# Order of DVE and ACT work around the pairs and levels of the second attention

## The chip, the cores and the metric

The kernel runs on one core of one Trainium2 chip. The metric is the device time in microseconds of one execution, the median of repeated runs. The engines are TensorE (PE), VectorE (DVE), ScalarE (ACT), GpSimd (POOL) and SyncE (SP), which issues the loads.

## The reference

Two transformer-like blocks run one after the other on 256 tokens of width 1024, each with a mixer and an expert layer over 16384 experts. The mixer of the second block is what matters here. It splits one input projection seven ways, into queries, keys and values of a block-sparse attention (8 heads of 64) and query, forget gate, input and output gate of a gated recurrence (4 heads of 128):

```
q_a, k_a, v_a, q_r, f_r, i_r, g_r = jnp.split(proj, IN_SPLITS, axis=-1)
attn = moba_attention(q_a.reshape(B, S, ATTN_HEADS, ATTN_HD),
...
rec = hgrn2(q_r, f_r, i_r, g_r, lb_all[layer], rec_norm_g[layer])
h = h + jnp.concatenate([attn, rec], axis=-1) @ w_out[layer]
```

With 256 tokens there is one attention block, so the attention is a causal softmax with a linear distance penalty. The recurrence is

```
decay = jnp.where(causal[None, None, :, :, None], jnp.exp(jnp.minimum(diff, 0.0)), 0.0)
scores = jnp.einsum('bhtd,bhtsd,bhsd->bhts', qc, decay, kc)
```

with `diff` the difference of cumulated logarithms of the forget gate. Its result is normed per head and multiplied with the opened output gate.

## The kernel before

All products run in float32 as three products of rounded halves. A weight tile of 128x1024 comes into one of four places of `ring`; ACT rounds it into `whi` (`highs_to`, L1232), POOL subtracts to get the rest `wlo` (L568), and PE multiplies high by high, low by high and high by low (L634 to L636). `highs_to(end)` rounds all tiles up to `end` that are not yet rounded; each rounding waits until PE has used the tile four before it. The roundings of slot s feed slot s + 2.

The second attention is the stage of this change. Its input projection has 14 slots (`IN2_SLOTS`): fr, fr, qr, qr, qa, ka, va, qa, ka, va, ir, ir, gr, gr, each of two weight tiles and 48 matmuls of 256 columns on PE. Slots of fr, qr, qa and ka come out as columns and are copied by DVE (L1853); va, ir and gr come out as rows and are copied by ACT (L1355, L1356).

Between the slots stand two chains of small work. **Pairs** (four pairs of heads): `m_scores` makes the scores on PE (L913, L915), DVE adds the penalty (L1862) and takes the maxima (L1864, L1865), ACT does four exponentials (L1364); `m_norm` is a reciprocal on DVE (L1868) and four scalings on ACT (L1371); `m_turn` turns the weights on PE (L924), ACT copies them (L1376); `m_values` multiplies by the values on PE (L888), ACT copies (`chi`, L1379), DVE takes the rest (`clo`, L1857). The turn of a pair waits for the `clo` of the pair before, since both use bank 1 of PSUM. **Levels** (0 to 8, doubling spans of the recurrence): `rec_decay` subtracts on DVE (L1884; level 8 L1887) and, in the same step, does two exponentials on ACT (L1388, L1389; level 8 L1391, L1392); `rec_factors` multiplies queries and keys by them on DVE (L1906, L1907; level 8 L1910, L1911); `rec_level` makes score matmuls in two halves on PE (L941, 16 records; level 8 L947); `rec_take` merges them into `Ssum` on DVE (L1894, twice). Level 8 is copied into `Sx` by ACT (L1395), and `rec_values` (L957, L960) needs `Sx`, all takes and the input slots. Then the norm, the gate (L1927) and the output projection follow.

The order is written out by hand: `schedule2` returns one list of steps, and each engine walks through the same list and emits its own part of each step. There is no scheduler behind it. So a step's place in the list is its place in the queue of each engine that has a part in it, and an instruction that waits holds up everything behind it on its engine. `SCORES_AT` puts the pairs' scores at slots 6, 7, 9 and 11, `LEVEL_AT` the levels 0 to 7 at slots 4 to 11; turn and scalings of a pair come one slot after its scores, its values two slots after.

Of the kernel before, what the change touches and what calls it, by code (L numbers as in the profile page):

```python
# [46 lines left out]
HALVES = KC // KH  # L47
RING = 4
# [40 lines left out]
FIRST, N_SLOTS = {}, 0  # L89
# [65 lines left out]
def schedule2():  # L155

    steps = []
    for s in range(len(IN2_SLOTS)):

        def pairs(late):  # L160
            return [h for h in range(PAIRS) if SCORES_AT[h] + late == s]

        level = s - LEVEL_AT[0] if s in LEVEL_AT else None
        if s == LEVEL_AT[-1] + 1:
            steps.append(("rec_level", 8))
        for h in pairs(1):
            steps.append(("m_norm", h))
        if level is not None:
            steps.append(("rec_factors", level + 1))
        if s == len(IN2_SLOTS) - 1:  # L170
            steps.append(("rec_norm", 0))
            steps.append(("proj_half", s))
            for h in pairs(2):
                steps.append(("m_values", h))
        steps.append(("proj", s))
        if s == 1:
            steps.append(("rec_prep", 0))
        if s == 2:
            steps.append(("rec_sums", 0))
        if s == 3:  # L180
            steps.append(("rec_decay", 1))
        if s < len(IN2_SLOTS) - 1:
            for h in pairs(2):
                steps.append(("m_values", h))
        if level is not None:
            steps.append(("rec_level", level))
            steps.append(("rec_take", level))
        if s == 12:
            steps.append(("rec_values", 0))
        for h in pairs(1):  # L190
            steps.append(("m_turn", h))
        for h in pairs(0):
            steps.append(("m_scores", h))
        if level is not None and level + 2 <= 8:
            steps.append(("rec_decay", level + 2))
    steps.append(("rec_gate", 0))
    return steps


def block_program(nc, weights, const1, const2, gains, keys_in, x, out):  # L200
    with ExitStack() as ctx:
# [299 lines left out]
        def bank(i, a=0, b=512):  # L501
            return ps[:, i, a:b]
# [690 lines left out]
        def _(eng):  # L1193
            steps = [0]
# [26 lines left out]
            def token_scale(t):  # L1221
                return stat[:, 3, t:t + 1]
# [3 lines left out]
            def highs_to(end):  # L1226

                for m in range(split[0], end):
                    eng.wait_ge(slot_in[m % RING], 16 * (m // RING + 1))
                    if m >= RING:  # L1230
                        eng.wait_ge(slot_used, m - RING + 1)
                    eng.activation(whi[:, m % RING, :], ring[:, m % RING, :], ACT.Copy).then_inc(hi_ready[m % RING], 1)  # L1232
                split[0] = end
# [97 lines left out]
            def attention2():  # L1331
                base = FIRST_GATE
                for what, i in schedule2():
                    if what == "proj_half":
                        highs_to(FIRST["in2"] + HALVES * i + 1 + RING)
                    elif what == "proj":
                        name, off = IN2_SLOTS[i]
                        if IN2_COLUMNS[i]:
                            highs_to(FIRST["in2"] + HALVES * (i + 1) + RING)
                            if name in FUNC:  # L1340
                                eng.wait_ge(col_copied, i + 1)
                                dst = colT[name][:, off // P:off // P + 2, :]
                                eng.activation(dst, dst, FUNC[name]).then_inc(fr_open if name == "fr" else qr_open, 1)
                            if name == "fr":
                                if i == 0:
                                    eng.wait_ge(g_lb, 1)
                                eng.wait_ge(fr_open, i + 1)
                                for h in (2 * i, 2 * i + 1):
                                    f = colT["fr"][:, h, :]
                                    eng.activation(f, f, ACT.Identity, bias=lbs[:, 6, h:h + 1], scale=lbs[:, 7, h:h + 1])\  # L1350
                                       .then_inc(fr_bound, 1)
                        else:
                            eng.wait_ge(slot_used, FIRST["in2"] + HALVES * (i + 1))
                            out, func = bank(4 + i % 2).rearrange("p (t c) -> p t c", t=2), FUNC.get(name, ACT.Copy)
                            eng.activation(raw2[name][:, 0, off:off + SC], out[:, 0, :], func, scale=token_scale(0))  # L1355
                            eng.activation(raw2[name][:, 1, off:off + SC], out[:, 1, :], func, scale=token_scale(1))\  # L1356
                               .then_inc(proj_copied, 1)
                            highs_to(FIRST["in2"] + HALVES * (i + 1) + RING)
                    elif what == "m_scores":
                        eng.wait_ge(m_max, i + 1)  # L1360
                        for h in range(2):
# [18 lines left out]
                    elif what == "rec_prep":  # L1380
                        eng.wait_ge(fr_bound, REC_H)
                        eng.activation(dlt.rearrange("p h t c -> p (h t c)"), colT["fr"].rearrange("p h c -> p (h c)"),
                                       ACT.Ln).then_inc(g_log, 1)
                    elif what == "rec_decay":
                        eng.wait_ge(g_dlt, i)
                        if i < 8:
                            v, h = level(dlt, i)
# [861 lines left out]
```

## Time and profile before

| | us |
|---|---|
| median of three runs | 2029.32 |
| lowest, highest | 2029.26, 2030.48 |
| the profiled execution | 2028.86 |
| its span in the profile | 2027.1 |
| window over slots 4 to 13 of the second attention | 94.0 |

The page gives each engine's busy share and the chain that ended last. A window gives busy time in a stretch, so that the gaps of an engine are the difference to its length. A timeline row is an instruction or a run of equal ones in order of time; in brackets stands how long the engine was idle before it and what ended that. PE's ends are modelled, each matmul's tail overlaps the next, so gaps are best read between starts.

### The profile page before, as it was taken

To read this page: it belongs to the slowest core of one execution; us is meant where nothing else is said; L and a number is where in the kernel's file an instruction comes from. 1 tells how busy PE (TensorE), PEld (TensorE's weight loads), DVE (VectorE), ACT (ScalarE), POOL (GpSimd) and SP (SyncE) were. 2 spreads that over 40 slices of the span, in tenths; PEclk is the share of its full clock that TensorE was granted. 3 is DMA by queue.
4 is the path that set the end of the run, shared out by engine and by line. 5 is a ranking of instruction groups with operands and counts; after the bars stand their busy time and mean duration, and the time that the engine had idled before them with its cause. 6 is when DMAs were issued, how large, how long until landed. Compare 5 with 4: busy or idle time off the path is not lost.

```text
span 2027.1 us, 39389 instructions
## 1 busy us (share of the span) xinstructions
PE 2000.8 (99%) x14308; PEld 1794.7 (89%) x14308; DVE 1236.9 (61%) x2093; ACT 1011.5 (50%) x1318; POOL 1420.0 (70%) x592
## 2 busy tenths in 40 slices
PE   8999999999999999999999999999999999999998
PEld 8988999999888888888889899999988888888886
DVE  5246379912776799953336638981276689994333
ACT  5546555454555544445446665444455544444443
POOL 7656878888877877754448467888877887774442
PEclk9999999999999999999999999999999999999999
DMA  7433545555555555565655344555555555555553
GB/s 267 157 126 125 186 150 184 180 183 178 174 172 172 174 173 170 175 224 186 186 187 178 114 146 148 188 184 183 180 166 175 176 170 172 172 169 182 185 187 129
DMA packets 97299, 351.46 MB, mean 173 GB/s; under 512 B 12113, under 2 KB 12369, under 8 KB 96849
## 3 DMA queue, kind: packets, MB, share of 16 engines
q1 hardware_dynamic: 96224, 345.40, 52.2%
q10 hardware_dynamic: 1008, 5.13, 0.7%
q8 instruction: 47, 0.77, 0.2%
q14 instruction: 20, 0.16, 0.0%
HBM read 349.44 MB, written 1.05 MB: 173 GB/s over the span
## 4 chain that ended last, share of the span: by engine, by line
PE 94%; DVE 3%; ACT 2%; issue 1%; DMA 0%; POOL 0%; SPq 0%; ACTq 0%; DVEq 0%; POOLq 0%
PE ps L634 23%; PE ps L636 23%; PE ps L635 23%; PE ps L1053 12%; PE ps L1054 6%; PE ps L1045 3%; PE ps L1029 1%; DVE act L1884 0%; PE ps L602 0%; DVE act L1907 0%; ACT whi L1232 0%; POOL wlo L577 0%; PE ps L779 0%; DVE act L1894 0%; DMA xres<-in_x 0%
## 5 line engine op out<-in xcount | busy, mean ns | idle before, releaser
L568 POOL TENSOR_TENSOR wlo<-ring,whi 128x1024 fp32r<-128x1024 f32 x584 | 1411.8, 2422 | 575.3 <-ACT whi L1421 455.9
L1421 ACT ACTIVATE whi<-ring 128x1024 fp32r<-128x1024 f32 x536 | 566.3, 1060 | 775.1 <-PE ps L636 588.7
L634 PE MATMUL ps<-whi,shi 128*128 128x512 f32 x1024 | 408.6, 399 | 0.0
L636 PE MATMUL ps<-whi,slo 128*128 128x512 f32 x1024 | 405.9, 396 | 0.0
L635 PE MATMUL ps<-wlo,shi 128*128 128x512 f32 x1024 | 405.9, 396 | 0.0
L634 PE MATMUL ps<-hboth,whi 128*128 128x256 f32 x1392 | 395.6, 284 | 0.0
L635 PE MATMUL ps<-hboth,whi 128*128 128x256 f32 x1392 | 393.9, 283 | 0.0
L636 PE MATMUL ps<-hboth,wlo 128*128 128x256 f32 x1392 | 393.9, 283 | 0.0
L1053 PE MATMUL ps<-hboth,whi 128*128 128x512 f32 x1024 | 359.3, 396 | 0.0
L1054 PE MATMUL ps<-hboth,wlo 128*128 128x256 f32 x1024 | 283.7, 277 | 0.0
L634 PEld LDWEIGHTS ps<-hboth,whi 128*128 128x128 f32 x1392 | 267.1, 192 | 1.4 <-issue 0.8
L635 PEld LDWEIGHTS ps<-hboth,whi 128*128 128x128 f32 x1392 | 267.2, 192 | 0.0
L636 PEld LDWEIGHTS ps<-hboth,wlo 128*128 128x128 f32 x1392 | 267.1, 192 | 0.0
L636 PEld LDWEIGHTS ps<-whi,slo 128*128 128x128 f32 x1024 | 192.8, 188 | 46.8
L634 PEld LDWEIGHTS ps<-whi,shi 128*128 128x128 f32 x1024 | 192.9, 188 | 45.6
L635 PEld LDWEIGHTS ps<-wlo,shi 128*128 128x128 f32 x1024 | 193.0, 189 | 45.4
L1053 PEld LDWEIGHTS ps<-hboth,whi 128*128 128x128 f32 x1024 | 192.1, 188 | 43.1
L2057 DVE TENSOR_TENSOR wlo<-ring,whi 128x1024 fp32r<-128x1024 f32 x64 | 79.7, 1245 | 238.0 <-ACT whi L1421 238.0
L2051 DVE TENSOR_TENSOR slo<-act,shi 128x512 fp32r<-128x512 f32 x128 | 183.9, 1437 | 22.4 <-ACT shi L1485 22.4
L1054 PEld LDWEIGHTS ps<-hboth,wlo 128*128 128x128 f32 x1024 | 192.4, 188 | 0.0
L2013 DVE TENSOR_TENSOR work<-iota,ps 128x1024 f16<-128x1024 f16 x128 | 154.9, 1210 | 0.0
L2023 DVE TENSOR_TENSOR act<-ps,act 128x512 f32 (+1 forms) x128 | 86.9, 682 | 95.2 <-PE ps L1045 95.2
(300 smaller groups left out, 2709.2 us busy)
## 6 DMA issues: line engine op xcount, KB each, us to landing
ring<-in_weights SPq DMA_DIRECT2D x651, 512.0 KB, 3.3
act<-in_const ACTq DMA_DIRECT2D x1, 2372.0 KB, 9.1
act<-in_const SPq DMA_DIRECT2D x1, 2240.0 KB, 12.3
xres<-in_x SPq DMA_DIRECT2D x4, 256.0 KB, 4.5
act<-in_keys ACTq DMA_DIRECT2D x1, 1024.0 KB, 4.8
out<-act ACTq DMA_DIRECT2D x2, 512.0 KB, 2.6
ring<-in_weights SPq DMA_DIRECT2D x2, 256.0 KB, 4.7
act<-in_fgain ACTq DMA_DIRECT2D x1, 512.0 KB, 3.5
```

Source lines behind the costliest of these rows:

```text
L568: pool.tensor_tensor(wlo[:, j, :], ring[:, j, :], whi[:, j, :].bitcast(F32), ALU.subtract)\
L634: pe.matmul(dst, wide[0], narrow[0], start=start, stop=False, skip_group_check=True)
L635: pe.matmul(dst, wide[0], narrow[1], start=False, stop=False, skip_group_check=True)
L636: return pe.matmul(dst, wide[1], narrow[0], start=False, stop=stop, skip_group_check=True)
L1045: mm = pe.matmul(bank(6 + c, q * HALF, (q + 1) * HALF), hot2[:, c, q, :], hot1[:, c, w, q, :], start=(q + w == 0), stop=(w == 1), skip_gro ...
L1053: pe.matmul(bank(b), whi[:, j, c], hboth[:, :, kc, :], start=kc == 0, stop=False, skip_group_check=True)
L1054: mm = pe.matmul(bank(b, 0, S), wlo[:, j, c], hhi[:, kc, :], start=False, stop=kc == KC - 1, skip_group_check=True)
L1421: eng.activation(whi[:, j, :], ring[:, j, :], ACT.Copy).then_inc(hi_ready[j], 1)
L2013: eng.tensor_tensor(hot2[:, j], iota[:, :].unsqueeze(1).to_broadcast([P, TOK, NKEY]), over(row(1, at), NKEY), ALU.is_equal)
L2023: eng.tensor_tensor(a, bank(6 + j).rearrange("p (q k) -> p k q", q=TOK), a, ALU.mult)\
L2051: eng.tensor_tensor(slo[:, j, :, :], act[:, bass.ds(p * 2, 2), :], shi[:, j, :, :].bitcast(F32), ALU.subtract)\
L2057: eng.tensor_tensor(wlo[:, j, :], ring[:, j, :], whi[:, j, :].bitcast(F32), ALU.subtract)\
```

## The change

Five steps of `schedule2` get other places. The roundings of a slot (`highs_to`) become a step of their own, `highs`, behind the values of a pair; they used to follow the slot's own copy. `m_norm` moves from the next slot to the end of the slot of its scores. ACT's part of `rec_decay` becomes a step of its own, `rec_exp`, behind the scalings. `rec_factors` of level l + 1 moves from the head of the next slot to behind the take of level l, or, in a slot with scores, to behind them; at level 8 it stands ahead of the scores. The first half of slot 12 moves ahead of level 8 (`proj_half`), and the rounding that belongs to it ahead of the copy of level 8. No instruction is added or taken out.

```diff
--- before.py
+++ after.py
@@ -162,11 +162,8 @@
 
         level = s - LEVEL_AT[0] if s in LEVEL_AT else None
         if s == LEVEL_AT[-1] + 1:
+            steps.append(("proj_half", s))
             steps.append(("rec_level", 8))
-        for h in pairs(1):
-            steps.append(("m_norm", h))
-        if level is not None:
-            steps.append(("rec_factors", level + 1))
         if s == len(IN2_SLOTS) - 1:
             steps.append(("rec_norm", 0))
             steps.append(("proj_half", s))
@@ -179,20 +176,29 @@
             steps.append(("rec_sums", 0))
         if s == 3:
             steps.append(("rec_decay", 1))
+            steps.append(("rec_exp", 1))
         if s < len(IN2_SLOTS) - 1:
             for h in pairs(2):
                 steps.append(("m_values", h))
+        steps.append(("highs", s))
         if level is not None:
             steps.append(("rec_level", level))
             steps.append(("rec_take", level))
         if s == 12:
             steps.append(("rec_values", 0))
+        if level == 7:
+            steps.append(("rec_factors", 8))
         for h in pairs(1):
             steps.append(("m_turn", h))
         for h in pairs(0):
             steps.append(("m_scores", h))
+        if level is not None and level < 7:
+            steps.append(("rec_factors", level + 1))
+        for h in pairs(0):
+            steps.append(("m_norm", h))
         if level is not None and level + 2 <= 8:
             steps.append(("rec_decay", level + 2))
+            steps.append(("rec_exp", level + 2))
     steps.append(("rec_gate", 0))
     return steps
 
@@ -1336,8 +1342,8 @@
                     elif what == "proj":
                         name, off = IN2_SLOTS[i]
                         if IN2_COLUMNS[i]:
-                            highs_to(FIRST["in2"] + HALVES * (i + 1) + RING)
                             if name in FUNC:
+                                highs_to(FIRST["in2"] + HALVES * (i + 1) + RING)
                                 eng.wait_ge(col_copied, i + 1)
                                 dst = colT[name][:, off // P:off // P + 2, :]
                                 eng.activation(dst, dst, FUNC[name]).then_inc(fr_open if name == "fr" else qr_open, 1)
@@ -1355,7 +1361,8 @@
                             eng.activation(raw2[name][:, 0, off:off + SC], out[:, 0, :], func, scale=token_scale(0))
                             eng.activation(raw2[name][:, 1, off:off + SC], out[:, 1, :], func, scale=token_scale(1))\
                                .then_inc(proj_copied, 1)
-                            highs_to(FIRST["in2"] + HALVES * (i + 1) + RING)
+                    elif what == "highs":
+                        highs_to(FIRST["in2"] + HALVES * (i + 1) + RING)
                     elif what == "m_scores":
                         eng.wait_ge(m_max, i + 1)
                         for h in range(2):
@@ -1381,7 +1388,7 @@
                         eng.wait_ge(fr_bound, REC_H)
                         eng.activation(dlt.rearrange("p h t c -> p (h t c)"), colT["fr"].rearrange("p h c -> p (h c)"),
                                        ACT.Ln).then_inc(g_log, 1)
-                    elif what == "rec_decay":
+                    elif what == "rec_exp":
                         eng.wait_ge(g_dlt, i)
                         if i < 8:
                             v, h = level(dlt, i)
```

DVE at slots 5 to 7, before: the decay of level 3 (L1884), the factors of level 3 (L1906, L1907), the take of level 2 (L1894), the scores of pair 0 (L1862 to L1865), the decay of level 4, the reciprocals of pair 0, the factors of level 4.

```order
L1884 TENSOR_TENSOR act<-act 128x1024 [waits rec_level_ready]
L1906 TENSOR_TENSOR act<-act 128x128x4 [waits rec_scores_ready,rec_exp_ready]
L1907 TENSOR_TENSOR act<-act 128x128x4
L1894 COPY_PREDICATED act<-act,ps 128x512 [waits rec_scores_ready] x2
L1862 SCALAR_TENSOR_TENSOR act<-ps,act 128x768 [waits moba_scores_ready]
L1864 TENSOR_REDUCE stat<-act 128x2 [waits dve_step]
L1865 TENSOR_REDUCE stat<-act 128x2
L1884 TENSOR_TENSOR act<-act 128x1024 [waits rec_level_ready]
L1868 RECIPROCAL stat<-stat 128x2x2 [waits moba_exp_ready]
L1906 TENSOR_TENSOR act<-act 128x64x8 [waits rec_scores_ready,rec_exp_ready]
L1907 TENSOR_TENSOR act<-act 128x64x8
```

The same place after (L1891 decay, L1901 take, L1869 to L1872 scores, L1913 and L1914 factors, L1875 reciprocals):

```order
L1891 TENSOR_TENSOR act<-act 128x1024 [waits rec_level_ready]
L1901 COPY_PREDICATED act<-act,ps 128x512 [waits rec_scores_ready] x2
L1869 SCALAR_TENSOR_TENSOR act<-ps,act 128x768 [waits moba_scores_ready]
L1871 TENSOR_REDUCE stat<-act 128x2 [waits dve_step]
L1872 TENSOR_REDUCE stat<-act 128x2
L1913 TENSOR_TENSOR act<-act 128x128x4 [waits rec_scores_ready,rec_exp_ready]
L1914 TENSOR_TENSOR act<-act 128x128x4
L1875 RECIPROCAL stat<-stat 128x2x2 [waits moba_exp_ready]
L1891 TENSOR_TENSOR act<-act 128x1024 [waits rec_level_ready]
```

The factors of level 3 moved from ahead of the take to behind the maxima of pair 0, and the reciprocals ahead of the decay of level 4.

ACT at slots 7 and 8, before: the exponentials of level 5 (L1388, L1389), the scalings of pair 1 (L1371), the roundings of slot 8 (L1232), the copy of pair 0's values (L1379), the copy of pair 1's turned weights (L1376).

```order
L1388 ACTIVATE act<-act 128x32x16 [waits rec_diff_ready]
L1389 ACTIVATE act<-act 128x32x16
L1371 ACTIVATE act<-act,stat 128x128 [waits moba_reciprocal_ready]
L1371 ACTIVATE act<-act,stat 128x256
L1371 ACTIVATE act<-act,stat 128x128
L1371 ACTIVATE act<-act,stat 128x256
L1232 ACTIVATE whi<-ring 128x1024 [waits slot_used,slot_in0]
L1232 ACTIVATE whi<-ring 128x1024 [waits slot_used,slot_in1]
L1379 ACTIVATE chi<-ps 128x256 [waits moba_out_ready]
L1376 ACTIVATE act<-ps 128x768 [waits moba_out_ready,moba_transposed]
```

The same place after (L1378 scalings, L1395 and L1396 exponentials, L1386 values, L1238 roundings, L1383 turned weights):

```order
L1378 ACTIVATE act<-act,stat 128x128 [waits moba_reciprocal_ready]
L1378 ACTIVATE act<-act,stat 128x256
L1378 ACTIVATE act<-act,stat 128x128
L1378 ACTIVATE act<-act,stat 128x256
L1395 ACTIVATE act<-act 128x32x16 [waits rec_diff_ready]
L1396 ACTIVATE act<-act 128x32x16
L1386 ACTIVATE chi<-ps 128x256 [waits moba_out_ready]
L1238 ACTIVATE whi<-ring 128x1024 [waits slot_used,slot_in0]
L1238 ACTIVATE whi<-ring 128x1024 [waits slot_used,slot_in1]
L1383 ACTIVATE act<-ps 128x768 [waits moba_out_ready,moba_transposed]
```

The values' copy now stands ahead of the roundings and right behind the exponentials, which stand behind the scalings.

DVE at slots 10 to 12, before: factors of level 7, take of level 6, decay of level 8 (L1887), factors of level 8 (L1910, L1911), rest of pair 2's values (L1857), take of level 7, scores of pair 3.

```order
L1906 TENSOR_TENSOR act<-act 128x8x64 [waits rec_scores_ready,rec_exp_ready]
L1907 TENSOR_TENSOR act<-act 128x8x64
L1894 COPY_PREDICATED act<-act,ps 128x512 [waits rec_scores_ready] x2
L1887 TENSOR_TENSOR act<-act 128x4x128 [waits rec_level_ready]
L1910 TENSOR_TENSOR act<-act 128x4x128 [waits rec_scores_ready,rec_exp_ready]
L1911 TENSOR_TENSOR act<-act 128x4x128
L1857 TENSOR_TENSOR clo<-ps,chi 128x256 [waits heads_highs_ready]
L1894 COPY_PREDICATED act<-act,ps 128x512 [waits rec_scores_ready] x2
L1862 SCALAR_TENSOR_TENSOR act<-ps,act 128x768 [waits moba_transposed,moba_scores_ready]
L1864 TENSOR_REDUCE stat<-act 128x2 [waits dve_step]
L1865 TENSOR_REDUCE stat<-act 128x2
```

The same place after (L1894 decay of level 8, L1917 and L1918 factors of level 8, L1864 rest of the values):

```order
L1901 COPY_PREDICATED act<-act,ps 128x512 [waits rec_scores_ready] x2
L1913 TENSOR_TENSOR act<-act 128x8x64 [waits rec_scores_ready,rec_exp_ready]
L1914 TENSOR_TENSOR act<-act 128x8x64
L1894 TENSOR_TENSOR act<-act 128x4x128 [waits rec_level_ready]
L1864 TENSOR_TENSOR clo<-ps,chi 128x256 [waits heads_highs_ready]
L1901 COPY_PREDICATED act<-act,ps 128x512 [waits rec_scores_ready] x2
L1917 TENSOR_TENSOR act<-act 128x4x128 [waits rec_scores_ready,rec_exp_ready]
L1918 TENSOR_TENSOR act<-act 128x4x128
L1869 SCALAR_TENSOR_TENSOR act<-ps,act 128x768 [waits moba_transposed,moba_scores_ready]
L1871 TENSOR_REDUCE stat<-act 128x2 [waits dve_step]
L1872 TENSOR_REDUCE stat<-act 128x2
```

The factors of level 8 moved from ahead of the take of level 7 to between it and the scores of pair 3.

## Rows read from the trace of the kernel before

**Rows 1.** the page: busy time of the span, and the chain by engine

```profile
PE 2000.8 (99%) x14308; PEld 1794.7 (89%) x14308; DVE 1236.9 (61%) x2093; ACT 1011.5 (50%) x1318; POOL 1420.0 (70%) x592
...
PE 94%; DVE 3%; ACT 2%; issue 1%; DMA 0%; POOL 0%; SPq 0%; ACTq 0%; DVEq 0%; POOLq 0%
```

**Rows 2.** windows view: us, then busy us of PE, PEld, DVE, ACT, POOL, clock, DMA

```profile
1093.00:1187.00 94.00, 90.97 (x768) 86.93 (x767) 61.40 (x78) 58.73 (x115) 57.43 (x23) 1.00 0.38 125
```

**Rows 3.** PE timeline: start, length, line, operands, count, [idle before, releaser]

```profile
1123.12 1.95 PE L941 MATMUL ps<-act 128*128 128x128 f32 x16
...
1125.76 0.87 PE L924 MATMUL ps<-ident,act 128*128 128x128 f32 x6 [0.70 <-ACT act L1371]
...
1134.16 2.05 PE L941 MATMUL ps<-act 128*128 128x128 f32 x16
...
1137.91 0.84 PE L924 MATMUL ps<-ident,act 128*128 128x128 f32 x6 [1.69 <-DVE clo L1857]
...
1153.92 1.95 PE L941 MATMUL ps<-act 128*128 128x128 f32 x16
...
1155.70 0.82 PE L924 MATMUL ps<-ident,act 128*128 128x128 f32 x6
...
1166.56 1.13 PE L947 MATMUL ps<-act 128*128 128x128 f32 x8 [0.65 <-DVE act L1894]
...
1173.28 1.28 PE L957 MATMUL ps<-act 128*128 128x128 f32 x10
```

**Rows 4.** POOL timeline of the same stage: the low roundings of the slots

```profile
1088.56 24.70 POOL L568 TENSOR_TENSOR wlo<-ring,whi 128x1024 fp32r<-128x1024 f32 x8 [1.45 <-ACT whi L1232]
...
1117.28 2.42 POOL L568 TENSOR_TENSOR wlo<-ring,whi 128x1024 fp32r<-128x1024 f32 x1 [4.02 <-ACT whi L1232]
...
1119.63 2.42 POOL L568 TENSOR_TENSOR wlo<-ring,whi 128x1024 fp32r<-128x1024 f32 x1
...
1146.39 4.74 POOL L568 TENSOR_TENSOR wlo<-ring,whi 128x1024 fp32r<-128x1024 f32 x2 [5.50 <-ACT whi L1232]
...
1157.21 4.77 POOL L568 TENSOR_TENSOR wlo<-ring,whi 128x1024 fp32r<-128x1024 f32 x2 [6.08 <-ACT whi L1232]
```

**Rows 5.** DVE timeline of the same stage: operations with two SBUF inputs

```profile
1108.11 2.87 DVE L1907 TENSOR_TENSOR act<-act 128x512 f32<-128x512 f32 x1
...
1119.93 3.21 DVE L1884 TENSOR_TENSOR act<-act 128x1024 f32<-128x1024 f32 x1
...
1124.96 0.68 DVE L1907 TENSOR_TENSOR act<-act 128x512 f32<-128x512 f32 x1
...
1151.05 1.22 DVE L1884 TENSOR_TENSOR act<-act 128x1024 f32<-128x1024 f32 x1
...
1159.84 2.69 DVE L1910 TENSOR_TENSOR act<-act 128x512 f32<-128x512 f32 x1 [2.60 <-ACT act L1392]
```

**Rows 6.** ACT and DVE timelines: exponentials 3, the maxima of scores 0 and 3

```profile
1114.38 0.63 ACT L1388 ACTIVATE act<-act 128x512 f32<-128x512 f32 x1 [5.84 <-DVE act L1884]
...
1119.33 0.68 DVE L1865 TENSOR_REDUCE stat<-act 128x2 f32<-128x512 f32 x1
...
1166.92 0.94 DVE L1862 SCALAR_TENSOR_TENSOR act<-ps,act 128x768 f32<-128x768 f32 x1
...
1168.23 0.68 DVE L1865 TENSOR_REDUCE stat<-act 128x2 f32<-128x512 f32 x1
```

**Rows 7.** ACT timeline: roundings of slot 8 and the copy of pair 0's values

```profile
1135.05 1.99 ACT L1232 ACTIVATE whi<-ring 128x1024 fp32r<-128x1024 f32 x2
...
1136.94 0.36 ACT L1379 ACTIVATE chi<-ps 128x256 fp32r<-128x256 f32 x1
```

**Rows 8.** ACT timeline: exponentials, cross copy and scalings at pair 3

```profile
1168.94 0.40 ACT L1364 ACTIVATE act<-act,stat 128x128 f32<-128x128 f32 x1 [3.63 <-DVE stat L1865]
...
1170.71 0.58 ACT L1395 ACTIVATE act<-ps 128x512 f32<-128x512 f32 x1
...
1171.19 1.49 ACT L1371 ACTIVATE act<-act,stat 128x128 f32<-128x128 f32 x4
```

## The prediction, made before the run

> **What bounds the kernel now.** I read the page first: TensorE (PE) is busy for 99% of the span and carries 94% of the chain that ended last [rows 1]. A change can therefore only help by closing a gap on PE, and it hurts as soon as it opens one. The change touches nothing but the second attention, so the next view is one window over that stage: 90.97 us of PE work in 94.00 us, at a granted clock of 1.00, the upper of its two levels [rows 2]. There are 3.0 us of gaps, and no more. The PE timeline says where they lie [rows 3]: 0.70 us before the turn of pair 0 (L924), which waits for the pair's scalings on ACT; 1.69 us before the turn of pair 1, which waits for the low rest of pair 0's values (clo) on DVE; 0.65 us before the scores of level 8 (L947), which wait for DVE's take of level 7. Counted from start to start, which also takes in the tail of the last matmul, a level block lasts 1155.70 - 1153.92 = 1.78 us where nothing waits, so the three waits cost 0.9 us (1123.12 to 1125.76), 2.0 us (1134.16 to 1137.91) and 0.65 us: **3.5 us in all, 0.17% of the run**. That is the most that the change can give back. A difference under about 0.2% (4.1 us) can't be told from no change here.
>
> **What the waits of the new order will be made of.** The second thing to read is how DVE and POOL hinder each other. DVE's subtraction of level 7 (L1884) took 1.22 us at 1151.05, when POOL's pair of roundings was ending at 1151.13; the same instruction for level 4 began at 1119.93 and took 3.21 us [rows 5]. POOL's second operation of that pair ran from 1119.63 to 1122.05 [rows 4], and DVE ended 1.1 us after it. The factors L1907 took 0.68 us beside an idle POOL, 2.87 us in the stretch in which POOL was busy without a break (1088.56 to 1113.26), and L1910 began at 1159.84, ended at 1162.53, and POOL's pair ended at 1161.98 [rows 4, 5]. So each of these operations with two inputs in SBUF waits until the POOL operation that is under way is over, and then needs about 0.55 us (512 elements) or 1.1 us (1024). POOL's eight operations in the long stretch lasted 24.70/8 = 3.1 us where 2.4 is usual: it waits for DVE as well. From the 2.87 us of the second of two factors I take that the two engines take turns, POOL's next operation slipping in between two of DVE's.
> The Trainium skill (SBUF — State Buffer, section "SBUF: two separate sides") calls this an exclusive lock on a shared port pair: who starts first keeps it for the whole instruction. The trace agrees. It speaks against this change, and without it the sum would be the gain of the last rival below.
>
> **The change, part by part.** A rounding pair on ACT takes 2.0 us [rows 7], and POOL's pair starts 1.1 us after the first and lasts 4.8 us. In the old order the factors of a level (L1906, L1907) stood at the head of the next slot, before the copy of its product: they ran when the exponentials ended, mostly after POOL's pair (levels 4 to 7 at 0.7 us each). In the new order they stand behind the take and, in a slot with a pair, behind the pair's maxima. That is 3 to 6 us after a slot's products end, just where POOL works on the pair of roundings that the same end released. No instruction is added or removed and no DMA issue moves; what changes is who waits. I carried the rows along the new order: an instruction starts when its engine is free and its releaser done, its length from the rows, port as above. The same working for the old order comes within 0.6 us of the trace at the end of the stage.
> - **Values ahead of the roundings.** Removes one rounding pair, 1.9 us, between the values' matmuls and their copy L1379: it ran at 1136.94, behind roundings from 1135.05 [rows 7]. The roundings are 0.4 us later, and have some 7 us until PE wants them: cost nothing.
> - **Scalings ahead of the exponentials.** Pair 0's scalings no longer stand behind a decay of 3.21 us and two exponentials of 1.2 us. The wait before turn 0 goes.
> - **Factors of level 3 behind scores 0.** First the delay before it: factors 2 and decay 3 now fall into POOL's pair of slot 5. Decay 3 ends at 1116.6 (before: 1114.35), its exponentials at 1117.8, and they hold up the copy of slot 6 and its roundings: POOL starts at 1119.5 instead of 1117.28 [rows 4, 6]. Maxima 0 end at 1119.9, as before (1120.01) [rows 6]. Factor one finds POOL at work until 1121.9, ends at 1122.5; POOL's second operation lasts until 1124.7; factor two ends at 1125.3. Level 3 was reached at 1123.12 [rows 3]: **a new wait of 2.2 us**. The order of the two requests at 1119.5 and 1119.8 is close.
> - **Turn 1.** Factors 4 end at 1134.7, decay 5 at 1136.0, exponentials 5 at 1137.4. Values 0 end at 1135.5, but their copy now stands behind exponentials 5: clo at 1138.1, where level 4 is over at 1137.1. The wait shrinks from 2.0 to **1.0 us** and does not go.
> - **Level 6** (factors behind scores 2, POOL's pair up to 1153.6): factors end 1154.8, PE is there at 1154.1: **0.7 us**, new.
> - **Level 8.** Half a slot of products (2.9 us: level 8 and a whole slot take 1173.28 - 1166.56 = 6.7) now stands ahead of it, which covers the take. But factors 8 come after take 7, not at 1159.84. Roundings 11 start at 1164.5, POOL at 1165.6; factor one asks at 1166.7 and ends at 1168.6, POOL's second operation at 1170.8, factor two at 1171.4. PE is through at 1169.8: **1.6 us** instead of 0.65.
> - **The cross copy Sx (L1395).** Scores 3 now wait behind factors 8: 0.96 for the sum, 1.0 for the maxima, 1173.3; exponentials 1.8; reciprocals 0.2; scalings 1.4, which before stood behind Sx (1170.71, then 1171.19) and now ahead of it; a rounding, 1.0; Sx 0.6 [rows 6, 8]: 1178.4. The values matmuls (1173.28 before) are ready at 1171.4 + 0.9 + 2.9 = 1175.2: **3.2 us**, new.
> From there to the end of the stage each engine keeps its distance to PE: the last gate and the turns move as a whole.
> Sum: 2.2 + 1.0 + 0.7 + 1.6 + 3.2 = 8.7 us of waits for 3.5 before: **+5.2 us**. The profiled execution took 2028.86 us and its span 2027.1; the 1.8 us around it don't change, so it would be 2034.1. The median of the runs is 0.46 above: **2034.5 us**. Bounds: a factor pair that misses POOL costs 1.4 us, one that hits two of its operations up to 0.55 + 2.4 + 2.4 + 0.3, so each of the first, third and fourth terms may be off by up to 2 us where the order of requests flips; much of that comes back at the next level, whose factors then collide.
>
> **The rivals.**
> - **One collision fewer**: factors 8 get in before POOL's second operation, or factors 3 before its first and the next level does not pay. Against it: factors 8 ask 1.1 us after POOL's start; for it: 0.3 us at level 3. It saves 2.2 to 2.8 us: 2032.0. Not slower by the bound.
> - **One collision more**, at level 2 or 4 (at level 4 factors end 0.7 us before PE comes): +1.2 us, 2035.7.
> - **The waits go and nothing takes their place.** This is the other side: if DVE's operations were not held by POOL, every factor pair would take 1.4 us, level 3 to level 8 would find them ready, and only Sx would be late, by 1.4 us (2.8 less than above, with level 8 on time). 3.5 - 1.4 = 2.1 us are gained: 2027.2. It decides from the point at which factors 3 end before 1123.1 and factors 8 before 1169.8. Against it stand the five rows of DVE beside POOL [rows 5].
> - That the change does nothing on PE I leave out: the wait before turn 0 hangs on a queue place that is moved.
>
> **How the numbers follow.** Forecast 0.70 (own range 2033.4 to 2035.5), one collision fewer 0.12, one more 0.10, waits gone 0.08. Slower by over 4.1 us, above 2033.4: 0.67 + 0.10 = 0.77, the 0.03 left of the forecast being its low edge, where errors of 0.1 us add up along five chains. Within 0.2%: 0.03 + 0.12 + most of the 0.08 = 0.21. Faster by over 0.2% would need more than the 3.5 us that are there; I leave 0.02 for what this reading of the stage misses. The range 2031.5 to 2036.5 holds the forecast and both collision cases, and leaves the gain outside.
>
> **What would show it.** In the new profile: no wait at turn 0; a wait of about 2 us before level 3 (L947 there), released by the factors; about 1 us at turn 1 by clo; waits before level 8 and before the values matmuls (L963), the last by Sx at 3 us; factors at 2 to 3 us each where they took 0.7; PE's idle time in the stage at 7 to 8 us for 3.0. I am wrong if factors 3 and 8 take 0.7 us each, or if PE's gaps sum to under 4 us.

## The result: 6.7 us slower by the median, 5.3 us in the stage

The changed kernel took 2036.31 us (median of 7 runs, 2034.77 to 2039.42), the kernel before 2029.63 us beside it (7 runs, 2028.97 to 2030.68). The ratio is 1.0035, 95% interval 1.0025 to 1.0045: slower by more than the 0.2% that can be told. The direction was forecast, the size was not: the medians lie 6.7 us apart where 5.2 us were forecast. The profiled execution took 2034.77 us, its span 2033.0 us, 5.9 us more than before.

The page of the changed kernel, for [rows 1]:

```profile
PE 2002.9 (99%) x14308; PEld 1796.5 (88%) x14308; DVE 1245.9 (61%) x2093; ACT 1011.8 (50%) x1318; POOL 1419.3 (70%) x592
...
PE 95%; DVE 3%; ACT 1%; issue 1%; DMA 0%; POOL 0%; SPq 0%; DVEq 0%; ACTq 0%; POOLq 0%
```

PE is busy 2.1 us longer with the same 14308 matmuls. So idle time is not all: some work ran slower. The window over the stage, for [rows 2] (us, busy us of PE, PEld, DVE, ACT, POOL, clock, DMA share, GB/s), and three short ones behind level 3:

```profile
1093.00:1193.00 100.00, 93.68 (x773) 89.43 (x773) 70.84 (x78) 58.89 (x116) 57.91 (x23) 0.98 0.36 121
1125.00:1127.00 2.00, 0.91 (x4) 0.91 (x5) 2.00 (x3) 0.84 (x3) 0.49 (x1) 0.78 0.39 141
1127.00:1129.00 2.00, 2.00 (x11) 2.00 (x11) 1.63 (x3) 2.00 (x5) 0.00 (x0) 0.50 0.59 238
1129.00:1131.00 2.00, 2.00 (x19) 1.72 (x17) 0.75 (x1) 2.00 (x3) 1.28 (x1) 0.86 0.03 8
```

PE was idle for 6.3 us (before: 3.0; the prediction had 7 to 8), and behind the first long wait the granted clock stood at its lower level (0.50, 1.2 GHz), which the stage of before never shows. The PE timeline, for [rows 3] (start, length, line, operands, count, [idle before, releaser]; levels are L947 and L953 here, turns L930, the values matmuls L963):

```profile
1126.09 3.68 PE L947 MATMUL ps<-act 128*128 128x128 f32 x16 [2.04 <-DVE act L1914]
...
1139.84 0.82 PE L930 MATMUL ps<-ident,act 128*128 128x128 f32 x6
...
1155.84 1.98 PE L947 MATMUL ps<-act 128*128 128x128 f32 x16
...
1172.24 1.16 PE L953 MATMUL ps<-act 128*128 128x128 f32 x8 [1.33 <-DVE act L1918]
...
1179.22 1.38 PE L963 MATMUL ps<-act 128*128 128x128 f32 x10 [2.95 <-ACT act L1402]
```

Three of the five forecast waits are there; those at turn 1 and level 6 are not. Level 3 took 3.68 us where a level takes 1.95. DVE's factors at those two places, and POOL's roundings (for [rows 4, 5]):

```profile
1120.45 2.82 DVE L1913 TENSOR_TENSOR act<-act 128x512 f32<-128x512 f32 x1
1123.19 2.84 DVE L1914 TENSOR_TENSOR act<-act 128x512 f32<-128x512 f32 x1
...
1167.66 1.74 DVE L1917 TENSOR_TENSOR act<-act 128x512 f32<-128x512 f32 x1
1169.32 2.87 DVE L1918 TENSOR_TENSOR act<-act 128x512 f32<-128x512 f32 x1
```

```profile
1120.32 5.17 POOL L574 TENSOR_TENSOR wlo<-ring,whi 128x1024 fp32r<-128x1024 f32 x2 [4.02 <-ACT whi L1238]
...
1166.46 5.18 POOL L574 TENSOR_TENSOR wlo<-ring,whi 128x1024 fp32r<-128x1024 f32 x2 [1.37 <-ACT whi L1238]
```

The stage is best measured from the start of level 0 to that of the turns ahead of the output projection, since what lies before it differs by up to 2.6 us from one execution to the next. Before, and of the changed kernel:

```profile
1099.47 1.72 PE L941 MATMUL ps<-act 128*128 128x128 f32 x14
...
1186.23 1.04 PE L977 MATMUL ps<-ident,act 128*128 128x128 f32 x8
```

```profile
1100.25 0.94 PE L947 MATMUL ps<-act 128*128 128x128 f32 x7
...
1192.28 0.93 PE L983 MATMUL ps<-ident,act 128*128 128x128 f32 x7
```

That is 86.76 us and 92.03 us: **+5.27 us**. The forecast of the stage holds to 0.1 us, with a low clock in it that was not foreseen. A window over each of the two stages parts them into idle time and work:

```profile
1099.47:1186.23 86.76, 83.73 (x707) 79.69 (x705) 57.54 (x74) 53.53 (x108) 50.19 (x21) 1.00 0.38 123
```

```profile
1100.25:1192.28 92.03, 85.71 (x706) 81.46 (x705) 67.51 (x75) 53.64 (x108) 49.94 (x21) 0.98 0.35 117
```

PE is idle 3.3 us longer (6.3 for 3.0) and works 2.0 us longer on the same matmuls. Two things had to be settled: why the stage isn't longer for it, and what makes up the rest of the medians' difference.

### The profile page after: what moved, and what is told of

Its sections match the earlier page's. It is cut to its first block, busy times and chain, and to the rows that moved or that the text cites. A ratio compares the mean times of both kernels' runs of the same rounds, so it can differ in the third digit from the quotient of the medians.

```text
span 2033.0 us, 39389 instructions
## 1 busy us (share of the span) xinstructions
PE 2002.9 (99%) x14308; PEld 1796.5 (88%) x14308; DVE 1245.9 (61%) x2093; ACT 1011.8 (50%) x1318; POOL 1419.3 (70%) x592
## 4 chain that ended last, share of the span: by engine, by line
PE 95%; DVE 3%; ACT 1%; issue 1%; DMA 0%; POOL 0%; SPq 0%; DVEq 0%; ACTq 0%; POOLq 0%
PE ps L640 23%; PE ps L642 23%; PE ps L641 23%; PE ps L1059 12%; PE ps L1060 6%; PE ps L1051 3%; PE ps L1035 1%; PE ps L947 1%; DVE act L1914 0%; PE ps L608 0%; DVE act L1913 0%; PE ps L785 0%; POOL wlo L583 0%; DVE act L1891 0%; DMA xres<-in_x 0%
```

## The experiments

The medians of all of them, beside 26 to 30 runs of the kernel before in the same session. "Stage" is the length just defined, in the profiled execution; "low at" is where its clock was at 1.2 GHz (the last 7 us of every span left aside, where it is low in every trace).

| kernel | median | before | ratio, 95% interval | stage | to 86.76 | low at |
|---|---|---|---|---|---|---|
| e1 change again | 2036.03 | 2030.56 | 1.0028 (1.0017-1.0039) | 92.01 | +5.25 | 125 us, level 3 |
| e2 all factors back | 2028.64 | 2030.56 | 0.9994 (0.9985-1.0003) | 85.67 | -1.09 | none |
| e3 fillers in the stage | 2035.15 | 2030.56 | 1.0023 (1.0014-1.0032) | 91.96 | +5.20 | 125 us |
| e4 only values moved | 2028.40 | 2030.56 | 0.9989 (0.9980-0.9998) | 84.35 | -2.41 | 125 us |
| e5 before, filler at 125 us | 2029.70 | 2030.57 | 0.9999 (0.9990-1.0008) | 87.03 | +0.27 | none |
| e6 change, filler at 125 us | 2035.85 | 2030.57 | 1.0027 (1.0016-1.0037) | 93.85 | +7.09 | values |
| e7 only values, filler at 125 us | 2027.17 | 2030.57 | 0.9985 (0.9976-0.9994) | 84.42 | -2.34 | none |
| e8 change, POOL quiet | 2027.52 | 2030.57 | 0.9987 (0.9978-0.9996) | 84.83 | -1.93 | 125 us |
| e9 change, fillers at 125 us and values | 2034.83 | 2030.32 | 1.0023 (1.0014-1.0032) | 92.21 | +5.45 | none |
| e10 factors 8 back | 2031.88 | 2030.32 | 1.0007 (0.9998-1.0016) | 87.82 | +1.06 | level 3 |
| e11 only factors moved | 2042.06 | 2030.32 | 1.0059 (1.0043-1.0075) | 97.97 | +11.21 | 125 us, levels 3 and 8 |
| e12 before, POOL quiet | 2027.33 | 2030.32 | 0.9989 (0.9979-0.9998) | 84.57 | -2.19 | none |

**The change again, and the clock (e1, e3).** e1 has no edit. e3 puts work of no use into PE's long waits:

```
     elif what == "rec_level":
+        keep_busy({3: 12, 8: 8}.get(i, 0))    # transposes of ident into bank 0, columns 384 to 511
     ...
     elif what == "rec_values":
+        keep_busy(18)
```

> The changed kernel once more, as it is, for a second trace of it. Theory (waits plus clock): TensorE waits about 2 us before level 3, 1.3 us before level 8 and 3 us before the values matmuls, and behind one or both of the long waits its granted clock is at the lower level for some 3.4 us, which costs 1.7 us each time; 2034.8 to 2037.6 us by how often that happens, about 6.7 above the kernel before. Rival (waits alone): the low clock in the first trace was a single event; this trace shows 1.00 through the whole stage and the time is 5.2 above, 2034.5.

> The changed kernel with transposes of the identity into an unused piece of PSUM put on TensorE ahead of its waits at level 3 (12, about 1.7 us), level 8 (8, about 1.2 us) and the values matmuls (18, about 2.6 us). No wait gets shorter for it, the engine is only kept active while it waits. Theory (clock): the granted clock stays 1.00 in the stage, each low stretch that the changed kernel shows is gone, 1.7 us less for each: about 2034.5, and its runs lie closer together. Rival (waits alone): time unchanged, since the filler replaces idle time and nothing else. Third case: the filler itself is late by its tail and costs up to 0.5 us.

e1 shows the same three waits (2.02, 1.32, 2.95 us), the low clock behind the first, and one more that the first trace had not: at 125 us, in the first attention. The wait there is in every trace without a filler at that place, of before too; what follows it is not always the same. Before, its PE row and two windows:

```profile
126.86 0.70 PE L841 MATMUL ps<-act 128*128 128x256 f32 x2 [2.12 <-DVE act L1770]
```

```profile
124.00:128.00 4.00, 1.88 (x14) 1.62 (x13) 3.96 (x5) 0.91 (x1) 2.35 (x1) 1.00 0.01 4
128.00:132.00 4.00, 4.00 (x35) 3.95 (x34) 0.96 (x2) 2.04 (x3) 2.38 (x1) 1.00 0.48 147
```

And e1, the same two views:

```profile
127.56 1.03 PE L847 MATMUL ps<-act 128*128 128x256 f32 x2 [2.13 <-DVE act L1777]
```

```profile
124.00:128.00 4.00, 1.87 (x14) 1.58 (x14) 3.28 (x4) 1.60 (x2) 2.32 (x1) 0.97 0.00 1
128.00:132.00 4.00, 4.00 (x20) 3.73 (x19) 1.51 (x3) 0.00 (x0) 2.38 (x2) 0.60 0.39 135
```

The same wait to 0.01 us; once 35 matmuls in the next 4 us, once 20, which is 1.6 us of work less. That is paid in full: in the fourteen traces level 0 of the second attention begins at 1099.5 to 1100.3 us where the clock stayed high at 125 us, and at 1101.2 to 1102.0 us where it was low. e3's fillers held the clock at 1.00 through the whole stage, but my expectation for its length was wrong: 91.96 us, not 1.7 us less. The 1.7 us went into waits that came back, 0.64 at turn 1 and 0.48 at level 6. The median fell by 0.9 us against e1. That suggests that some runs had held a low stretch that the fillers took away and the traces so far did not show; with 7 and 11 runs that spread over 2.9 and 2.7 us it is not shown by this.

**Which low stretch costs (e5, e6, e9).** e5 and e6 are before and the change, with this ahead of the wait at 125 us; e9 is e6 with the 18 transposes of e3 ahead of the values matmuls:

```
     elif what == "sb_later":
+        for _ in range(14 if i == 0 else 0):
+            pe.transpose(bank(0, 384, 512), ident[:, :], ident[:, :])
         pe.wait_ge(stay_ready, i + 1)
```

> The kernel before, with 14 transposes of the identity into an unused piece of PSUM ahead of TensorE's first wait in the first attention (2.12 us at 125 us, released by DVE). In three of the six traces so far the granted clock was at the lower level for some 3.2 us right behind this wait, in three it was not. Theory: that is what parts the runs of every kernel here into two groups 1.6 us apart; with the engine active the low stretch never comes, all runs lie in the lower group, median 2029.2. Rival: the groups have another origin; both are still there, median 2030.5.

> The changed kernel with the same 14 transposes at 125 us and nothing in the second attention. Theory: the runs lose the 1.6 us of the first attention; 2034.6 where only the wait before level 3 is followed by a low clock, up to 2036.2 where the 2.95 us wait before the values matmuls is too. Median 2034.6, that is 5.4 above the kernel before with the same filler. Rival: the surplus over 5.2 that the first runs showed is due to the change; median 2036.

> The changed kernel with the 14 transposes at 125 us and 18 more ahead of TensorE's wait before the values matmuls (2.94 us); nothing at level 3. In the profiled run with the filler at 125 us alone the clock was low behind the values wait and the stage was 1.8 us longer than where it was low behind level 3. Theory: a low stretch behind level 3 is paid out of the waits at turn 1 and level 6 and costs nothing, one behind the values wait costs 1.7 in full; so all runs come to one group, 5.3 above the lower group of before: 2034.5, none above 2035.5, whether or not the clock is low behind level 3. Rival: the low stretch at level 3 costs too; runs remain at 2036 and above.

In e5 the two groups of before (13 of 30 runs at 2028.8 to 2029.9, the others at 2030.4 and above) became one, 2028.87 to 2030.18. Its median is 0.5 above what I expected; its stage is 0.27 longer, with 0.98 us before turn 0 for 0.70; why is open. In e6 three of eight runs lay at 2034.0 to 2034.9, four at 2035.8 to 2036.8, one at 2037.58. The median, 2035.85, is the rival's figure and not the expected 2034.6: I had taken a low clock behind the values wait for the exception. This time the trace caught that case. Its PE rows:

```profile
1125.64 1.61 PE L949 MATMUL ps<-act 128*128 128x128 f32 x12 [2.13 <-DVE act L1916]
...
1138.58 0.85 PE L932 MATMUL ps<-ident,act 128*128 128x128 f32 x6 [0.66 <-DVE clo L1866]
...
1155.21 2.05 PE L949 MATMUL ps<-act 128*128 128x128 f32 x16 [0.47 <-DVE act L1916]
...
1171.70 1.16 PE L955 MATMUL ps<-act 128*128 128x128 f32 x8 [1.32 <-DVE act L1920]
...
1178.67 1.89 PE L965 MATMUL ps<-act 128*128 128x128 f32 x10 [2.95 <-ACT act L1404]
```

Its windows behind level 3 and behind the values wait:

```profile
1127.00:1131.00 4.00, 4.00 (x36) 3.50 (x35) 3.43 (x6) 3.83 (x6) 1.74 (x1) 1.00 0.23 91
...
1178.00:1182.00 4.00, 3.33 (x18) 3.33 (x19) 0.00 (x0) 3.97 (x7) 2.55 (x2) 0.67 0.11 15
1182.00:1186.00 4.00, 4.00 (x33) 4.00 (x32) 1.22 (x1) 2.84 (x4) 2.17 (x1) 0.90 0.45 146
```

All five forecast waits are there, since the clock stayed high behind level 3, and it was low behind the values wait, where 4 x 0.33 + 4 x 0.10 = 1.7 us are lost. Nothing that waits stands behind that place, so the stage is 93.85 us. A low stretch behind level 3, on the other hand, is made good by level 6: level 6 begins 55.6 us behind level 0 in the change, whose clock was low, and 55.7 in e6, whose clock was high there. With the filler there too (e9) all eleven runs lay at 2034.24 to 2035.43. Level 3 still has its wait, a filler stands ahead of the last:

```profile
1126.19 2.05 PE L954 MATMUL ps<-act 128*128 128x128 f32 x16 [2.12 <-DVE act L1922]
...
1176.11 2.13 PE L903 MATMUL ps<-ident 128*128 128x128 f32 x18
...
1179.22 1.38 PE L971 MATMUL ps<-act 128*128 128x128 f32 x10 [0.98 <-ACT act L1410]
```

e9 against e5, the two kernels without the chance stretches: 2034.83 - 2029.70 = 5.1 us.

**Which part of the change costs (e2, e4, e10, e11).** e2 and e10 are the change with factors put back to where they stood before. That is the head of the slot of level l for the factors of level l + 1, one slot after their decay: the change put them later within this slot, from ahead of its projection to behind its take or scores. e4 is before with the roundings (`highs_to`) moved behind `m_values` in all slots but those of fr and qr, e11 is before with both moves of `rec_factors` alone:

```
 e2, in schedule2 (e10 for level 7 alone):
+        if level is not None:
+            steps.append(("rec_factors", level + 1))      # ahead of ("proj", s)
 e4:
+        steps.append(("highs", s))                        # behind m_values, the only difference to before
```

> The changed kernel with the factors of all levels put back to the head of the next slot (the rest of the change stays). Theory: the moved factors make the waits before levels 3 and 8 and the late cross copy; by the rows carried along the order, waits of 2.2 us at turn 1 and 0.6 us before the values matmuls stay, no wait at levels 3, 6 and 8, clock 1.00 but perhaps behind turn 1; 1 us below the kernel before, 2028.4. Rival: the scalings or the values' copy ahead of the roundings cost time of themselves; then it stays 2 us or more above the kernel before.

> The kernel before with one part of the change alone: a pair's values copied ahead of the slot's roundings. Theory: clo of pair 0 comes 1.9 us earlier, the wait of 1.7 us at turn 1 shrinks to 0.2, the wait of 0.7 at turn 0 stays, level 8 is not late; 2.0 to 2.6 us less than before, 2027.0 to 2027.6, a version ahead of both. Rival: the roundings that are moved behind the copy come late for the products or push a decay behind POOL's pair; then the time is that of before or up to 2 us more.

> The changed kernel with the factors of level 8 alone put back ahead of the projection of slot 11. Theory: no wait before level 8, the pair's maxima 3 no longer stand behind factors 8 and the cross copy comes some 3.5 us earlier; the waits at level 3 (2.1), turn 1 (0.7) and level 6 (0.5) stay, that before the values matmuls falls to about 0.6. Some 4.2 us less than the change: 1.0 above the kernel before, 2031.6. Rival: the cross copy is late because of the scalings ahead of it, not because of the factors; then the wait before the values stays near 2 us, 2033 or more.

> The kernel before with the factors alone moved (levels 1 to 7 behind the pair's scores, level 8 behind the take), all else in the old order. Theory: this part is what costs; the waits at level 3, 6, 8 and before the values matmuls come, and the scalings and the values' copy aren't there to give something back: 9 us above the kernel before by the carried rows, 2039.5, up to 1.7 more where the clock falls behind a wait. Rival: the parts are independent and the rest of the change gives 1 to 2.6 us; then 6 to 8 us above.

With the factors back nothing is late at levels 3, 6 and 8; 1.59 us at turn 1 and 0.35 before the values stay, and the stage is 1.09 us shorter than before (expected 1.0). So the factors' move accounts for 92.03 - 85.67 = 6.4 us beside the other moves, and these give 1.1 without it. Of the 6.4 us, factors 8 alone are 92.03 - 87.82 = 4.2 us, as expected; e10's last PE row:

```profile
1174.84 1.38 PE L963 MATMUL ps<-act 128*128 128x128 f32 x10 [0.34 <-ACT act L1402]
```

The wait of 2.95 us before the values has fallen to 0.34, with the scalings still ahead of Sx. e10 is also a second case of a low clock behind level 3 that costs nothing: no wait at turn 1 nor at level 6, and 1.06 us where 1.0 was carried. e4 gave 2.4 us; the waits at turn 1 and before level 8 are gone, that at turn 0 (0.69) stays. e11 was a miss by 0.5 to 2.2 us (11.2 in the stage). The waits at level 3 (2.04 us) and level 8 came, those at level 6 and before the values matmuls did not. Without the half slot ahead of it level 8 waited for the factors for longer than any place of the change, and the clock fell behind that wait as well:

```profile
1177.62 2.08 PE L949 MATMUL ps<-act 128*128 128x128 f32 x8 [4.13 <-DVE act L1913]
```

The stage of e11, and eight us behind level 3 in it:

```profile
1101.82:1199.79 97.97, 89.43 (x706) 84.38 (x705) 61.34 (x75) 53.53 (x108) 49.14 (x21) 0.93 0.33 110
1128.00:1136.00 8.00, 7.22 (x39) 5.94 (x38) 4.21 (x8) 5.12 (x9) 3.55 (x2) 0.57 0.22 68
```

PE is idle for 8.5 us (before: 3.0) and works for 89.4 us (before: 83.7). So of the 11.2 us, 5.5 are idle time and 5.7 slower matmuls. The low stretch behind level 3 loses 8 x 0.43 = 3.4 us less half of the 0.8 us in which PE is idle there, 3.0 us, where the others lose 1.7; the rest stands behind the wait of 4.13 us. How much of this took the place of waits is open. The parts don't add up: the other moves of the change give 1.1 us where the factors stay (e2) and 97.97 - 92.03 = 5.9 us where they are moved.

**Is it POOL? (e8, e12.)** The same edit in both kernels: in the second attention POOL rounds 64 of 1024 columns. The kernel leaves the rest of the low halves out; every instruction is there:

```
-                        pool.tensor_tensor(wlo[:, j, :], ring[:, j, :], whi[:, j, :].bitcast(F32), ALU.subtract)\
+                        pool.tensor_tensor(wlo[:, j, 0:64], ring[:, j, 0:64], whi[:, j, 0:64].bitcast(F32), ALU.subtract)\
```

> The changed kernel, but POOL's low roundings of the second attention cover only 64 of 1024 columns of a weight slot (the rest of the low halves is left as it was, so the products are computed with wrong low parts; the instructions of TensorE, DVE and ACT are all there). Theory (DVE waits for POOL's operation under way): the factors take 0.7 us each everywhere, the waits before levels 3, 6 and 8 go, only the cross copy stays late by 1.4 us at the values matmuls; the time falls by 7 to 7.5 us to about 2028. Rival (the place in DVE's row alone makes them late): the factors still end late, the waits at level 3 and 8 stay above 1 us, time above 2033.

> Control for the run with POOL quiet: the kernel before with POOL's low roundings of the second attention on 64 of 1024 columns (low parts of the products wrong). Theory: decay 3 and 4 take 1.2 us for 3.2, the wait before turn 0 goes (0.9), those at turn 1 (values' copy behind the roundings) and level 8 (take) are not POOL's and stay: 0.9 to 1.2 us below the kernel before, 2029.5. So with POOL quiet the change would be worth about 1 to 2 us and with POOL at work it costs 5.3. Rival: less work on POOL speeds every kernel by the same 7 us; 2023.5.

DVE and POOL in e8, at level 3 and the roundings before it:

```profile
1121.80 0.68 DVE L1917 TENSOR_TENSOR act<-act 128x512 f32<-128x512 f32 x1
1122.39 0.68 DVE L1918 TENSOR_TENSOR act<-act 128x512 f32<-128x512 f32 x1
```

```profile
1119.09 0.32 POOL L574 TENSOR_TENSOR wlo<-ring,whi 128x64 fp32r<-128x64 f32 x1 [7.88 <-ACT whi L1242]
1120.03 0.33 POOL L574 TENSOR_TENSOR wlo<-ring,whi 128x64 fp32r<-128x64 f32 x1 [0.62 <-ACT whi L1242]
```

The factors have the same place in DVE's row as in the change and take 0.68 us each. Of the waits one is left in the stage, by Sx:

```profile
1173.72 1.38 PE L967 MATMUL ps<-act 128*128 128x128 f32 x10 [1.30 <-ACT act L1406]
```

That is 1.30 us where 1.4 was worked out. The median lies 8.5 us below that of e1 and the stage 92.01 - 84.83 = 7.2 us, where 7 to 7.5 were expected. The place in the row alone is not what makes them late. But the theory of e12 was off: I expected 0.9 to 1.2 us, the stage gave 2.19. The wait at turn 1 was POOL's too, which I had put down to ACT's order alone. It is decay 5 that had held the exponentials, and they the roundings and the copy. Before, and in e12:

```profile
1129.46 3.12 DVE L1884 TENSOR_TENSOR act<-act 128x1024 f32<-128x1024 f32 x1
```

```profile
1129.09 1.22 DVE L1888 TENSOR_TENSOR act<-act 128x1024 f32<-128x1024 f32 x1
```

The wait at turn 1 in e12 is:

```profile
1136.27 0.85 PE L928 MATMUL ps<-ident,act 128*128 128x128 f32 x6 [0.43 <-DVE clo L1861]
```

With POOL quiet the two kernels differ by 84.83 - 84.57 = 0.26 us in the stage and 0.19 in the medians. So of the 5.3 us that the change costs in the stage, 5.0 exist only because POOL's roundings hold DVE.

**The better kernel (e7)**: e4 with the filler of e5.

> The kernel before with only the values' copy moved ahead of the roundings, and the 14 transposes at 125 us: the best of both findings. 2.4 us from the wait at turn 1, the low stretch at 125 us never there: median 2026.9, 3.6 below the kernel before. Rival: the filler costs what it saves; 2028.4 as without it.

2027.17 us (2026.9 expected), ratio 0.9985 (0.9976 to 0.9994), ahead of both kernels; against e5, which differs by the values' move alone, 2.5 us. ACT at slot 8, with chi ahead of the roundings (before they stood the other way round, [rows 7]), and PE's one wait left in the stage:

```profile
1135.76 0.36 ACT L1383 ACTIVATE chi<-ps 128x256 fp32r<-128x256 f32 x1
1136.02 2.00 ACT L1235 ACTIVATE whi<-ring 128x1024 fp32r<-128x1024 f32 x2
```

```profile
1126.47 0.87 PE L927 MATMUL ps<-ident,act 128*128 128x128 f32 x6 [0.79 <-ACT act L1375]
```

## The prediction, step by step

- **Bound and place of the loss**: right. The stage holds 5.3 of the 5.9 us of the spans; of the rest 0.8 lie ahead of level 0, where the kernels don't differ, and -0.2 behind the stage.
- **Collisions**: right. Shifted by the 0.78 us by which level 0 began later, factors 3 ended at 1122.5 and 1125.2 (forecast 1122.5 and 1125.3), factors 8 at 1168.6 and 1171.4 (the same), the values matmuls began at 1178.4 (the same).
- **The five waits**: forecast from start to start at 2.2, 1.0, 0.7, 1.6 and 3.2 us. Where the clock stays high (e6) the idle times are 2.13, 0.66, 0.47, 1.32 and 2.95. With the tails, which I estimate at 0.15 to 0.3 us each ([rows 3] give 0.2 and 0.3), they come to 8.3 to 9.0 us for 8.7.
- **Values' copy behind exponentials 5, scalings ahead**: right; the wait before turn 0 went, that at turn 1 shrank and stayed (e6).
- **The step that failed** is the sum. It takes the clock of the window of before, 1.00, for the stage of the change, though it has just put waits of 2.2 and 3.2 us into it. The missing term is a low stretch behind them. Behind level 3 it is worth 1.7 us and is paid out of the waits at turn 1 and level 6, whose releasers did not get later: 0 in the sum. That the stage of the first trace came to the forecast 5.2 us is partly luck: the low stretch fell where it is free, and in e6 the same order took 7.1 us more than before. Behind the values wait nothing follows that could pay: 1.7 us in part of the runs, by their times four or five of eight in e6 (one trace shows it). The median of e6 lies 1.0 us above that of e9, which differs by the filler there alone.
- **The median of the runs** failed with it. I added 0.46 us to the profiled time from three runs. By 29 runs the kernel before lies in two groups some 1.6 us apart, with few runs between them, by the clock behind the wait at 125 us, which has nothing to do with the change; three runs don't tell their shares. How many of the seven runs of the change had that stretch can't be read from their times, since both stretches cost the same. So the 6.7 us of the first comparison are 5.3 from the stage, and the rest from both stretches in shares that stay open. One run, 2039.42 us, lies 4.6 us above the lowest, more than two stretches of 1.7 us give, and no trace shows what it was; the second comparison gave 2036.03 - 2030.56 = 5.5.
- **The rival of the other side** ("the waits go"): its condition was tried, and the changed kernel came where the working put it: 2027.52 us for 2027.2, with a lone wait of 1.30 us by Sx. As a price of the change it was wrong: it kept the 3.5 us of the kernel before fixed, and 2.2 of these were POOL's as well (e12).
- The exclusive lock of the Trainium skill (SBUF — State Buffer, section "SBUF: two separate sides") is borne out by e8 and e12: with the order unchanged the factors of level 3 take 0.68 us instead of 2.8 (e8), and decay 5 takes 1.22 us instead of 3.12 (e12).

## What to carry to other kernels

On a stage where one engine works without a break, what a moved operation costs is read from what the *other* user of its port is doing at the new time, not from its own length: here 1.4 us of factors became 5.6. When a sum of waits is made, say behind each new wait of the sizes behind which the clock fell here (2.0 us and more) whether a wait follows that can pay for a low clock; if none does, the slower matmuls are a term of their own, present in part of the runs. Take a change of several moves apart before judging it: the move that was worth 2.4 us by itself (e4) was hidden under one that cost 6.4. And don't add the parts up: the factors' move cost 11.2 us without the others (e11).

## What the hardware showed that I had not expected

The granted clock can fall from 2.4 to 1.2 GHz behind a wait of just 2.02 us (e10). It mostly lost 1.6 to 1.7 us of matmul work each time, behind level 3 of e11 3.0 us, where shorter waits follow. It does not do so every time: behind the wait of 2.12 us at 125 us in five of the ten traces without a filler there (e1, e3, e4, e8, e11), and behind the wait before level 3 in four (the change, e1, e10, e11, waits of 2.02 to 2.04 us) and not in two (e6, e9, waits of 2.13 and 2.12 us). Behind the wait of 2.95 us before the values matmuls it fell in one trace (e6) and not in two (the change, e1). Twelve to eighteen useless transposes ahead of the wait kept it at 2.4 GHz in every trace in which they stood. The medians fell by them without any work less: by 0.9 us for before (e5, where the interval of the ratio, 0.9990 to 1.0008, still holds 1), 1.2 us for e4 (e7), 1.0 us for the change between e6 and e9.
